# A hybrid decoder trunk on one core: projections begin with four weight units per input chunk, and the up-projections use four accumulators

## The reference

```python
for i in range(DEPTH):
    hn = rmsnorm(x, norm_mix_pre[i])
    m = mamba2_mixer(hn, ...) if i % 2 == 0 else diff_attention(hn, ...)
    x = x + rmsnorm(m, norm_mix_post[i])
    hn = rmsnorm(x, norm_ffn_pre[i])
    f = conv_ffn(hn, ...)          # up to 2 x 2816, causal conv of width 3, silu(gate) * up, down
    x = x + rmsnorm(f, norm_ffn_post[i])
```

## Time and profile before

| what | value |
|---|---|
| median of 3 runs | 1554.38 us (1552.46 to 1554.84) |
| the profiled execution's own time | 1555.5 us |
| its span | 1553.3 us |
| TensorE busy in the span | 1467.8 us (94%) |
| VectorE busy | 1020.3 us (66%) |
| ScalarE busy | 613.7 us (40%) |
| GpSimd busy | 212.2 us (14%) |
| granted TensorE clock, mean | 0.979 of full |

### The profile page before, as it was taken

One profiled execution on the slowest core, in us unless ns is written; L12 is line 12 of the kernel. 1 busy time (PEld: TensorE's weight loads), 2 busy tenths in 40 slices (PEclk: granted clock), 3 DMA queues, 4 the chain that ended last, 5 costly groups with the idle time before them and its releaser, 6 DMA issues.

```text
span 1553.3 us, 20707 instructions
## 1 busy us (share of the span) xinstructions
PE 1467.8 (94%) x6774; PEld 1163.5 (75%) x6774; DVE 1020.3 (66%) x1417; ACT 613.7 (40%) x953; POOL 212.2 (14%) x134
## 2 busy tenths in 40 slices
PE   6889999999997999999999799999788999999996
PEld 5678888888785788888888577776566888888885
DVE  6769888889426877777422657778358777775223
ACT  5455555566324322222322345565433222223221
POOL 3000111111114000000011432322141000000111
PEclk9999999999998999999999999999889999999998
DMA  4333333332221222223222122111112222223221
GB/s 147 139 122 123 129 112 122 125 123 77 82 95 41 95 95 95 95 95 105 95 93 90 38 82 68 60 62 54 41 68 68 95 95 95 95 95 112 93 93 54
DMA packets 36274, 142.04 MB, mean 91 GB/s; under 512 B 4049, under 2 KB 4177, under 8 KB 34193
## 3 DMA queue, kind: packets, MB, share of 16 engines
q1 hardware_dynamic: 36240, 141.62, 26.9%
HBM read 139.38 MB, written 2.23 MB: 91 GB/s over the span
## 4 chain that ended last, share of the span: by engine, by line
PE 75%; issue 9%; DVE 9%; POOL 3%; ACT 2%; DMA 1%; SPq 0%; DVEq 0%; POOLq 0%; ACTq 0%
PE bank L354 23%; PE bank L355 23%; PE bank L356 23%; POOL w_lo L323 3%; DVE hn_lo L534 2%; DVE w_lo L330 2%; DVE mbuf L544 1%; DMA raw<-w_mix 1%; DVE x L560 1%; ACT w_hi L317 1%; PE b_y L731 1%; PE b_x L743 1%; DVE cv_s L715 1%; PE b_y L734 1%; PE b_norm L453 0%
## 5 line engine op out<-in xcount | busy, mean ns | idle before, releaser
L354 PE MATMUL bank<-hn_hi,w_hi 128*128 128x512 f32 x1288 | 522.9, 406 | 47.5 <-DVE hn_lo L534 36.6
L355 PE MATMUL bank<-hn_lo,w_hi 128*128 128x512 f32 x1288 | 513.4, 399 | 0.0
L356 PE MATMUL bank<-hn_hi,w_lo 128*128 128x512 f32 x1288 | 513.0, 398 | 0.0
L317 ACT ACTIVATE w_hi<-raw 128x1024 fp32r<-128x1024 f32 (+1 forms) x217 | 239.8, 1105 | 513.9 <-PE bank L356 487.9
L330 DVE TENSOR_TENSOR w_lo<-raw,w_hi 128x1024 fp32r<-128x1024 f32 (+1 forms) x194 | 258.7, 1334 | 262.4 <-ACT w_hi L317 261.8
L354 PEld LDWEIGHTS bank<-hn_hi,w_hi 128*128 128x128 f32 x1288 | 244.9, 190 | 122.6 <-issue 31.0
L356 PEld LDWEIGHTS bank<-hn_hi,w_lo 128*128 128x128 f32 x1288 | 244.6, 190 | 59.3
L355 PEld LDWEIGHTS bank<-hn_lo,w_hi 128*128 128x128 f32 x1288 | 245.3, 190 | 56.0
L356 PE MATMUL bank<-h_hi,w_lo 128*128 128x512 f32 x352 | 139.2, 396 | 0.0
L354 PE MATMUL bank<-h_hi,w_hi 128*128 128x512 f32 x352 | 139.2, 396 | 0.0
L355 PE MATMUL bank<-h_lo,w_hi 128*128 128x512 f32 x352 | 139.2, 396 | 0.0
(11 more groups left out here) (202 smaller groups left out, 1676.4 us busy)
## 6 DMA issues: line engine op xcount, KB each, us to landing
raw<-w_up SPq DMA_DIRECT2D x88, 512.0 KB, 3.3
raw<-w_mix SPq DMA_DIRECT2D x49, 512.0 KB, 3.3
raw<-w_dn SPq DMA_DIRECT2D x32, 704.0 KB, 4.0
raw<-w_qkv SPq DMA_DIRECT2D x24, 512.0 KB, 3.2
acs_bc<-scratch SPq DMA_DIRECT2D x8, 1024.0 KB, 4.6
ecs_bc<-scratch SPq DMA_DIRECT2D x8, 1024.0 KB, 4.7
raw<-w_sout SPq DMA_DIRECT2D x16, 512.0 KB, 3.3
raw<-w_aout SPq DMA_DIRECT2D x8, 512.0 KB, 3.3
```

The lines of the kernel that those rows point to most:

```text
L317: nc.scalar.activation(w_hi[:, slot, 0:ph.width], raw[:, slot, 0:ph.width], ACT.Copy).then_inc(hi_made, 1)
L354: nc.tensor.matmul(acc[:], wh, hi, start=first, stop=False)
L355: nc.tensor.matmul(acc[:], wh, lo, start=False, stop=False)
L356: return nc.tensor.matmul(acc[:], wl, hi, start=False, stop=last)
```

## The change

Where the next phase is one of `WIDE` (UP0, QKV, UP1), TensorE begins with units 0 to 3 together. Units 0 and 1 have weight buffers of their own (`fx_*`, `ax_*`), 2 and 3 the usual slots; units 0 and 1 accumulate in `b_y`, 2 and 3 in `b_x`. Of chunk 0 the eight matmuls that need only `hn_hi` come first. Chunks 1 to 5 are taken for all four units, then chunks 6 and 7 unit by unit in the order 2, 3, 0, 1, with the pre-norm's statistics after unit 2 and its broadcast after unit 0. The splits of the next phase's units 1 and 2 move into the last round of the output projection, ahead of the reading of its last two chunks; unit 3 is split where unit 1 was, unit 4 ahead of the pre-norm's root. VectorE's `scale(2)` comes after `lo(0)` instead of before it.

The up-projections then cycle over four banks (`bank[0]`, `bank[1]`, `b_x[0]`, `b_x[1]`). The loop handles two pairs a turn, and the split in the middle of a `conv` is that of the unit four further on. Attention's rounds 0 and 1 lose the four units that are done.

```diff
+        WIDE = (UP0, QKV, UP1)
...
+        def halves_of(ph, j, first=False):
+
+            if first and ph in WIDE and j < 2:
+                hi, lo = (ax_hi, ax_lo) if ph is QKV else (fx_hi, fx_lo)
+                return hi[:, j, 0:ph.width], lo[:, j, 0:ph.width]
+            slot = slot_of(ph, j)
+            return w_hi[:, slot, 0:ph.width], w_lo[:, slot, 0:ph.width]
...
+        def first_acc(ph, j):
+
+            return (b_x if j >= 2 else b_y)[:, j % 2, :] if ph in WIDE else acc_of(ph, j)
+
+        def up_acc(ph, j, first=False):
+
+            if first:
+                return first_acc(ph, j)
+            return b_x[:, j % 2, :] if j % 4 >= 2 else acc_of(ph, j)
...
+            if first and j < 2:
+                act.wait_ge(unit_done, ph.U0 - 2)
+            elif first and j in (2, 3, 4, 5):
+                act.wait_ge(unit_done, U - 3)
+            elif not (isinstance(j, int) and U < 2):
                 act.wait_ge(unit_done, U - 1)
...
+            if ph in (DN0, DN1) and isinstance(j, int) and j < 2:
+                pe.wait_ge(evac["in"], pv.before["in"] + pv.chunks - 3 + j)
...
+        def wait_up_bank(pe, ph, j):
+
+            pv = ph.prev
+            if isinstance(j, int) and j in (4, 5):
+                pe.wait_ge(evac["out"], pv.before["out"] + pv.chunks - 5 + j)
+            else:
+                pe.wait_ge(evac["in"], ph.before["in"] + j - 3)
...
+        def wide_start(pe, b, nxt):
+
+            def chunk(j, c):
+                return product(first_acc(nxt, j), 0, c, hn_hi[:, c, :], hn_lo[:, c, :], c == 0, c == KC - 1,
+                               halves_of(nxt, j, True))
+
+            pe.wait_ge(hnhi_ready, KC * b + 1)
+            for j in range(4):
+                pe.wait_ge(lo_made, nxt.U0 + j + 1)
+                wh, wl = halves_of(nxt, j, True)
+                nc.tensor.matmul(first_acc(nxt, j), wh[:, 0:P], hn_hi[:, 0, :], start=True, stop=False)
+                nc.tensor.matmul(first_acc(nxt, j), wl[:, 0:P], hn_hi[:, 0, :], start=False, stop=False)
+            pe.wait_ge(hnlo_ready, KC * b + 1)
+            for j in range(4):
+                nc.tensor.matmul(first_acc(nxt, j), halves_of(nxt, j, True)[0][:, 0:P], hn_lo[:, 0, :],
+                                 start=False, stop=False)
+            for c in range(1, KC - 2):
+                pe.wait_ge(hnlo_ready, KC * b + c + 1)
+                for j in range(4):
+                    chunk(j, c)
+            for n, j in enumerate((2, 3, 0, 1)):
+                for c in (KC - 2, KC - 1):
+                    pe.wait_ge(hnlo_ready, KC * b + c + 1)
+                    last = chunk(j, c)
+                last.then_inc(unit_done, 1)
+                if n == 0:
+                    wait_x_scaled(pe, b)
+                    sum_stat(pe, f"pre{b}")
+                elif n == 2:
+                    norm_bcast(pe, norm_no[f"pre{b}"])
...
             if b:
                 norm_root(act, norm_no[f"post{b}"])
                 if nxt is not None:
-                    split_hi(act, nxt, 1, 1)
+                    split_hi(act, nxt, 3, 3)
...
-            norm_root(act, norm_no[f"pre{b}"])
-            ahead(split_hi, act, nxt, 2)
+            if b:
+                split_hi(act, nxt, 4, 4)
+                norm_root(act, norm_no[f"pre{b}"])
...
-                if b and m and m + 1 < KC:
+                if b and 1 < m and m + 1 < KC:
                     scale(m + 1)
...
+                if b and m == 1:
+                    scale(2)
...
+            if last:
+                ahead(split, eng, ph, 4 * i + 5, 5)
+                ahead(split, eng, ph, 4 * i + 6, 6)
             chunk(2 * i, 0, 4 * i + 3)
...
         def ffn_pe(pe, up, dn, layer):
-            with pe.Fori(1, FC) as m:
-                in_unit(pe, up, 2 * m, 0)
-                in_unit(pe, up, 2 * m + 1, 1)
+            in_unit(pe, up, 4, 4)
+            in_unit(pe, up, 5, 5)
+            in_unit(pe, up, 6, 6)
+            in_unit(pe, up, 7, 7)
+            with pe.Fori(2, FC // 2) as i:
+                for r in range(4):
+                    in_unit(pe, up, 4 * i + r, r)
...
-            pair(0, True)
-            with act.Fori(1, FC - 1) as m:
-                pair(m)
-            pair(FC - 1)
+            pair(0, 5, 5, 6)
+            pair(1, 6, None, 7)
+            with act.Fori(1, FC // 2 - 1) as i:
+                pair(2 * i, 0, 4 * i + 4, 4 * i + 5)
+                pair(2 * i + 1, 2, 4 * i + 6, 4 * i + 7)
+            pair(FC - 2, 44, 2 * FC, 2 * FC + 1)
+            pair(FC - 1, 46)
...
+            pair(0, 0, 5, 6, True)
+            pair(1, 2, None, 7, True)
+            with dve.Fori(1, FC // 2 - 1) as i, ch.loop(i, 1, FC // 2 - 2, 4 * (FFN_T - 1)):
+                pair(2 * i, 0, 4 * i + 4, 4 * i + 5)
+                pair(2 * i + 1, 2, 4 * i + 6, 4 * i + 7)
+            pair(FC - 2, 0, 2 * FC, 2 * FC + 1)
+            pair(FC - 1, 2)
...
+            started = isinstance(h, int) and h == 0
+            starting = isinstance(h, int) and h == 1
+            if proj and not (started or starting):
                 in_unit(pe, QKV, 3 * h, rep)
+            if starting:
+                in_unit(pe, QKV, 3 * h + 1, rep + 1)
...
-                pe.wait_ge(evac["in"], QKV.before["in"] + 3 * h)
+                pe.wait_ge(evac["in"], QKV.before["in"] + 3 * h + (1 if starting else 0))
                 scores(0)
                 scores(1)
```

More of the change, by code:

```diff
@@ L349, in wait_bank, with product @@
                 pe.wait_ge(evac[ph.kind], ph.before[ph.kind] + j - 1)
-        def product(acc, slot, c, hi, lo, first, last):
-            wh, wl = w_hi[:, slot, c * P:(c + 1) * P], w_lo[:, slot, c * P:(c + 1) * P]
+        def wait_up_bank(pe, ph, j):
+            pv = ph.prev
+            if isinstance(j, int) and j in (4, 5):
+                pe.wait_ge(evac["out"], pv.before["out"] + pv.chunks - 5 + j)
+            else:
+                pe.wait_ge(evac["in"], ph.before["in"] + j - 3)
+        def product(acc, slot, c, hi, lo, first, last, weights=None):
+            wh, wl = weights or (w_hi[:, slot, :], w_lo[:, slot, :])
+            wh, wl = wh[:, c * P:(c + 1) * P], wl[:, c * P:(c + 1) * P]
             nc.tensor.matmul(acc[:], wh, hi, start=first, stop=False)
@@ L360, in in_unit @@
             pe.wait_ge(lo_made, ph.U0 + j + 1)
-            wait_bank(pe, ph, j)
+            if ph in (UP0, UP1):
+                wait_up_bank(pe, ph, j)
+                acc = up_acc(ph, rep)
+            else:
+                wait_bank(pe, ph, j)
+                acc = acc_of(ph, rep)
             for c in range(KC):
-                last = product(acc_of(ph, rep), slot_of(ph, rep), c, hn_hi[:, c, :], hn_lo[:, c, :],
+                last = product(acc, slot_of(ph, rep), c, hn_hi[:, c, :], hn_lo[:, c, :],
                                c == 0, c == KC - 1)
@@ L528, in boundary_pool @@
             if nxt is not None:
-                pool.wait_ge(lo_made, nxt.U0 + 3)
+                pool.wait_ge(lo_made, nxt.U0 + (5 if nxt in WIDE else 3))
         def boundary_dve(dve, b, nxt=None):
@@ L656, in out_wholes @@
             ahead(split, eng, ph, 2 * i + 2, 2)
+            if last:
+                ahead(split, eng, ph, 2 * i + 3, 3)
+                ahead(split, eng, ph, 2 * i + 4, 4)
             chunk(2 * i, 0, 2 * i + 1)
@@ L696, in out_phase_dve, with conv @@
             if nxt is not None:
-                split_lo_dve(dve, nxt, 0)
+                for j in range(3):
+                    split_lo_dve(dve, nxt, j)
             boundary_dve(dve, b, nxt)
-        def conv(dve, ph, j, rep, ug, taps, wcol, dst, n_conv, mid=None):
-            dve.wait_ge(unit_done, ph.U0 + j + 1)
+        def conv(dve, ph, j, rep, ug, taps, wcol, dst, n_conv, mid=None, first=False):
+            dve.wait_ge(unit_done, ph.U0 + j + (3 if first and j < 2 else 1))
             if not (isinstance(n_conv, int) and n_conv == 0):
                 dve.wait_ge(conv_ready, n_conv)
-            nc.vector.tensor_tensor(ug[:, taps - 1:taps - 1 + S], acc_of(ph, rep)[:], r_pre[:],
+            acc = up_acc(ph, rep, first) if ph in (UP0, UP1) else acc_of(ph, rep)[:]
+            nc.vector.tensor_tensor(ug[:, taps - 1:taps - 1 + S], acc[:], r_pre[:],
                                     ALU.mult).then_inc(evac["in"], 1)
@@ L1148, in ffn_dve @@
             dve.wait_ge(dve_done, ch.value())
-            pair(0, True)
-            with dve.Fori(1, FC - 1) as m, ch.loop(m, 1, FC - 2, 2 * (FFN_T - 1)):
-                pair(m)
-            pair(FC - 1)
+            pair(0, 0, 5, 6, True)
[5 more added lines that the diff above has]
+            pair(FC - 1, 2)
             hidden_lo(FC - 1)
@@ L1224, in att_pe @@
                 weights_back(3, "t3", h - 2)
-            if proj and not (isinstance(h, int) and h == 0):
+            if proj and not (started or starting):
                 in_unit(pe, QKV, 3 * h + 1, rep + 1)
@@ L1247, in att_pe @@
                 norm_stat(osq, 2)
-            if proj:
```

(12 more changed lines are left out.)

74 lines of the change are left out of this document (43 added, 31 removed).

## The result

The changed kernel takes 1545.79 us (median of 5, 1543.98 to 1547.92) against 1554.84 (5 runs, 1552.46 to 1555.68) for the kernel before: a ratio of 0.9941, with a 95% interval of 0.9929 to 0.9954. It is faster by 0.6%, 9.05 us where 17.4 were forecast, and lies at the upper end of the range. The profiled execution took 1544.31 us, its span is 1542.2 us.

A forecast was written before the change was run, and what follows sets the result against it. VectorE's chain was taken to bound the boundaries, TensorE the rest. Boundary gains 8.9 + 6.2 + 8.4, less 2 x 2.1, gave 19.3 us; less 2 for clock, 1538.2 profiled, so 1537 median, range 1530 to 1546.

The forecast's parts named there:

- What bounds the boundary: Boundaries: VectorE's scale, add and `lo` set the pace; work brought in is free until a chunk carries 2.5 us of products.
- The new waits: TensorE waits: 2.1 us at each down-projection's third unit, 2.6 before attention's unit 6, 0.5 for the third boundary's sum.
- The first rival: VectorE and ScalarE finish sooner, so no new waits appear: 26 us gained, 1528 to 1532; chance 0.13.
- The start of the up-projection and its loop: Up-projections: zero loss, though two margins are only 0.3 and 0.6 us; loop still 5.60 us a unit.
- The third: Boundaries: VectorE's chain stretches against GpSimd's sums and TensorE's reads, over 2.8 us a chunk: 1551 to 1557; chance 0.04.
- the fourth rival: Up loop: the later split comes too late in every pair, so slower; 1 us beyond gives 1577; chance 0.06.
- `scale(2)` behind `lo(0)` costs nothing: Boundary start on VectorE: the reordering costs zero, as chunk 1 decides, ready at 486.17 in the first boundary.
- nothing is added to that chain: Boundaries: argument against VectorE's chain needing 1.3 us more per chunk, though `lo` already takes 1.77 us beside GpSimd.
- and I take 2: Whole kernel: halved clock after the new waits costs 2 us, between zero and 8 at most.
- nearer to 1.6 than to 4.2: The new waits' lengths, compared with earlier waits followed by 1.00 (1.6 us) and 0.50 clock (4.2 us).
- If the same span follows the earlier start: First boundary, chunk 0: half clock lasts 3.73 us, all 12 products done by 486.1; gain 8.9 us.
- The second rival: Losses are larger: margins at units 6 and 7 fail, clock takes its 8 us: 1542 to 1548; chance 0.17.

The follow-up runs named there:

- the repetition: The changed kernel run again without any edit, beside other follow-up kernels: 1545.59 us, ratio 0.994.
- the early split: Changed kernel with the down-projection's third unit split ahead of the last hidden chunk and table load: 1536.28 us, ratio 0.9892.
- filler in the same wait: Changed kernel with eight useless products in front of the down-projection's third unit, in both layers: 1543.97 us, ratio 0.9938.

## Why the prediction was half right

**What bounds the boundary: right.** In both traces VectorE's chain sets it up to chunk 1, and work brought in from behind the boundary was all but free there. The first product comes 0.05 us after the first `hn_hi` (479.30 + 0.72), the eight early products are used, and behind chunk 1 TensorE doesn't wait again, as forecast.

**The new waits: right, in place and size.** 2.06 us twice, 2.71, and 0.40 and 0.55: the in-order chains of single rows gave each within 0.15 us, but for the 0.40 that was taken as covered. The first rival (they don't appear) is out.

**The start of the up-projection and its loop: right.** `lo(6)` ends at 516.8, wanted at 519.8; no wait for `w_lo` or `ug_f` at units 5 to 9, and 5.60 us a unit. The third and the fourth rival are out.

**The step that was mis-sized first: "`scale(2)` behind `lo(0)` costs nothing: the same instructions, and chunk 1, not chunk 0, decides".** The same instructions don't take the same time elsewhere. The sum took chunk 1 at 486.17 from the row of before, and in the changed kernel `lo(1)` starts 1.4 us later in its boundary: `lo(0)` takes 0.45 us more and the add 0.78 us more. By the run with the move undone it costs 0.9 to 1.4 us three times, 3.6 us. With 1.1 won before the change has any effect, 7.3 us are missing in the profiled execution (17.3 + 1.1 - 11.1). The three boundaries are short of the forecast by 4.35 of them, the clock took 1.9 beyond its term (below, less the 0.4 won back), the end of the kernel 0.8, and the two down-projection waits 0.2. The prediction even had the rule in hand, with `lo` at 1.77 us beside GpSimd, and added "nothing is added to that chain"; nothing was added, but it was moved. The Trainium skill (SBUF — State Buffer, "Who interferes with whom") says that a VectorE instruction with two SBUF inputs contends with a GpSimd instruction that reads SBUF, and one with at most one SBUF input, outside the two-port modes, doesn't. The traces agree: the add and `lo`, with two, go from 0.68 and 0.74 to 1.46 and 1.77 us, and `scale`, one of whose inputs is the PSUM tile `b_norm`, stays at 0.73 to 0.75 us beside the same work.

**The step that was mis-sized second: the clock's "and I take 2".** It took 3.1 behind the down-projections' waits and 1.2 behind unit 6 (154.75 us from the wait's end to the next wait at 1067.25, against 153.59 before): 4.3 us in this execution, within the bounds of 0 and 8. The waits were called "nearer to 1.6 than to 4.2", where full clock had followed the first; in the changed kernel a wait of 2.06 us was followed by half clock both times. Both kernels' run-to-run spread of 3 to 4 us is of the size of this term.

**A third size, hidden: "If the same span follows the earlier start, 8 or 9 products are done at 485.2, the other 3 or 4 by 486.1".** The half level did not end after 3.73 us. It lasted to the end of chunk 0 or close to it: 5.36 us at 0.53 for the 12 products in the changed kernel, where the sum has 4.7. With chunk 1 late this cost nothing; with the move undone it shows as 0.58 us in the first boundary and 0.49 in the third.

**The second rival.** The time lies in its band, 1542 to 1548, but it isn't what happened: its margins held, and the clock took about half of its 8. That the range held is in part luck: the repetition's trace and the first one's carry broadcasts of 1.12 or 2.07 us in the same place, and the median lies 0.2 us inside the upper bound.

## What to carry to other kernels

Before an instruction is called free because it only changes places, look at what the other engines do at its new time: here an add went from 0.68 to 1.46 us and a `lo` from 1.32 to 1.77 beside GpSimd, and it hurt only once the wide start had made TensorE the bound at that point. When a stall is removed from an engine, chain every producer that it will meet next from single rows (that worked within 0.15 us), and price each remaining gap of TensorE twice, once for its length and once for the clock behind it. Closing a gap by making its operand earlier gave the most (9.3 us for the early split, 1.8 for filler in the same wait); filler paid where the engine's next work was on the critical chain, as the broadcast is.
